# Conv half of the output projection's input normed early into its own tiles, two sums on TensorE, one more conditioning vector on GpSimd

## The chip, the cores and the metric

One NeuronCore of a Trainium2 chip runs the whole program. The metric is device time in microseconds (us) of one execution. TensorE is called PE in the profile, VectorE DVE, ScalarE ACT, GpSimd POOL and SyncE SP.

## What is computed

Two blocks of a network on x of 512 tokens and 1024 features, in float32. The change lies in the first block:

```python
cond = c_act @ ada_w[i] + ada_b[i]
shift1, scale1, gate1, shift2, scale2, gate2 = jnp.split(cond, N_MOD, axis=-1)
h = modulate(rmsnorm(x, norm1_g[i]), shift1, scale1)
u, v, val, gate = jnp.split(h @ w_in[i] + b_in[i], [D_A, 2 * D_A, 2 * D_A + D_B], axis=-1)
y_a = spatial_gating_mixer(gelu(u), gelu(v), ...)       # 512 features
y_b = conformer_conv_mixer(val, gate, ...)              # 512 features
y = jnp.concatenate([rmsnorm(y_a, out_norm_a_g[i]), rmsnorm(y_b, out_norm_b_g[i])], axis=-1)
x = x + gate1[:, None, :] * (y @ w_out[i])
h2 = modulate(rmsnorm(x, norm2_g[i]), shift2, scale2)
g_ff, up_ff = jnp.split(h2 @ w_ffn_in[i], 2, axis=-1)
x = x + gate2[:, None, :] * ((jax.nn.silu(g_ff) * up_ff) @ w_ffn_out[i])
```

At the end of the first block stands `shift_f, scale_f = split(c_act @ ada_f_w + ada_f_b)`. With the six vectors of `cond` these make eight conditioning vectors of 1024. The second block (attention, pooling, two feed-forward parts) is not touched.

## The kernel before

**Layout.** Features lie on the 128 partitions and the 512 tokens along the row, so 1024 features are 8 chunks of 128 x 512. A projection goes by blocks of 128 output features: a weight tile of 128 x 1024 is loaded (SyncE's queue, four tiles `raw` in turn), ScalarE rounds it into a high half (L293, `split_hi`), VectorE subtracts to get the low half (L297, `split_lo`), and TensorE makes three matmuls for each chunk (high x high, high x low, low x high), 24 for a block, into one of two banks in turn. The normed input has a high and a low half too. Blocks are numbered through: 0 to 15 are `w_in`, 16 to 23 `w_out`, 24 and on the first feed-forward part (`ffi0`, 44 blocks). `mm` counts blocks that TensorE has done, `wlo` splits that VectorE has done, `ev` the banks that were read out. Each engine works off its own list in the order in which the code writes it; nothing overtakes.

**Norms.** For a norm ScalarE squares each chunk, the squares are added up into one tile `ACC` (GpSimd, L575, for the norms `nb` of the conv half and `na` of the gated half; VectorE, L631, for `n2`), TensorE sums over the partitions by four matmuls with a column of ones (`pe_sum`, L476), VectorE makes the mean (L515), GpSimd the power -1/2 (L549), VectorE puts it on a diagonal (L524), and TensorE broadcasts that by a product with ones (`pe_bcast`, L493). Then, chunk by chunk, VectorE multiplies by gain and broadcast (L603), ScalarE writes the high half (L582, L584), VectorE the low half (L596, L598).

**Blocks 0 to 15** (TensorE from L1233, ScalarE from L1612, VectorE from L1976). Between the blocks stand the convolution, the group norm and the token mixing. In block 14 TensorE makes the mixing products `spatial` behind chunks 2 and 6. Ahead of block 14 stand the group-scale products (L1192), the second pair of which waits for VectorE's multiplies (L1974) of the first. In block 15 it sums `nb` behind chunk 0 and broadcasts it behind chunk 6.

**Blocks 16 and 17** (`first_two`, L1121) run staggered by three chunks, for the input is still being normed: chunks 4 to 7 (conv half, `nb`), then 0 to 3 (gated half, `na`), whose sum and broadcast stand at steps 3 and 4. Both halves are normed through the same two `TMP` tiles into `HH` and `HL`, which the blocks of `w_in` still read until block 15 is done, so the conv half is normed behind it.

**Blocks 18 to 23** (L1257, L1643, L2039). For each block VectorE splits the weight of the block after next, makes low halves for the lead blocks (`lead_low`, L2037), adds the gated result to the residual (L624), waits for its square (ScalarE, L651) and adds that to `ACC`, then does its conditioning steps.

**Lead phase** (`pe_phase_led`, L365). Blocks 24 and 25 are computed from the residual before its norm is known (`LH`, `LL`, L375 to L377); inside the first of them stand the sum for `n2` (behind chunk 2, its last part waits for the last square, L487) and its broadcast (behind chunk 6). The token factor is applied behind. Then blocks 26 and 27, staggered, read the normed chunks, and from block 28 on a loop runs.

**Conditioning vectors.** A vector is the sum of eight weight tiles (128 x 1024), each times a column of `c`: one step on VectorE for a tile (`ada_add`, L1897, L1910). `ADA_STEPS` (L39) lists how many steps VectorE does in each of its slots 0 to 15 and 16 to 23. Vectors 0 and 1 are made ahead of block 0 (L1878), 2 to 5 in these slots. Vectors 6 and 7 are made by GpSimd from the time when the lead norm is done: a load on its own queue, a product (L1019) and an addition (L1023) for each of 16 tiles, in `m_out`. For each vector TensorE sums over partitions (`ada_rows`, L1103), ScalarE copies the rows (`ada_flatten`, L1610), and TensorE turns them (`ada_turn`, L1111) into columns.

Of the kernel before, what the change touches and what calls it, by code (L numbers as in the profile page):

```python
# [14 lines left out]
F32 = mybir.dt.float32  # L15
# [23 lines left out]
ADA_STEPS = [2, 2, 1, 1, 1, 1, 1, 1, 2, 2, 2, 2, 2, 0, 0, 0] + [2, 2, 2, 2, 2, 1, 1, 0]  # L39
# [18 lines left out]
ADA_B = (ADA_N - 4) * C  # L58
ADA_C = 2 * C
PER = ADA_B // 16  # L60
# [13 lines left out]
def build_program(nc, xT, vec, ada_w, w_in, w_out, ffi, ffo, ln_rows, ws, bs, att_w, att_out, bf, pe, w1, w2,  # L74
                  pool_w, f2i, f2o, outT):
    ctx = ExitStack()
    with ctx:
# [30 lines left out]
        AE = [RAW[3][:, D:D + 2 * P], RAW[2][:, D:D + 2 * P]] + [HS[:, 0, 2 * P * i:2 * P * i + 2 * P] for i in range(2)]  # L108
# [92 lines left out]
        with ExitStack() as life:  # L201
            life.enter_context(nc.sbuf_tensor("final_lead_gap", [P, 2 * CF, S], F32))
            FLL = life.enter_context(nc.sbuf_tensor("final_lead_lo", [P, C, S], F32R))
            FSH = life.enter_context(nc.sbuf_tensor("final_shift_halves", [P, C, 2], F32R))
            FBI = life.enter_context(nc.sbuf_tensor("final_lead_bias", [P, 1], F32))
        with ExitStack() as life:
            for name, shape, dt in (("lead_gap0", [P, 14, S], F32), ("lead_hi_t", [P, C, S], F32R),
                                    ("lead_gap1", [P, 10, S], F32), ("lead_lo_t", [P, C, S], F32R),
# [68 lines left out]
        kinds = (("n1", C, 1, C - 1, C, C, C), ("nb", CA, 1, CA - 1, CA, CA, CA), ("na", CA, 1, CA - 1, CA, CA, CA),  # L277
# [87 lines left out]
        def pe_phase_led(name, hi, lo, ready, inside_lead, behind_lead, behind_first):  # L365
# [32 lines left out]
            behind_lead()  # L398
# [15 lines left out]
            behind_first()  # L414
            with nc.tensor.Fori(1, G[name]) as g:
# [531 lines left out]
        def _(pool):  # L947
# [68 lines left out]
            for i in range(ADA_C):  # L1016
                w, acc = LW[:, i % 2, :], LACC[:, i // C, :]
# [69 lines left out]
        def _(pe_):  # L1087
            def ada_sums(j, bank, sem_, count):

                pe_.wait_ge(sem_, count)  # L1090
                for k in range(C):
                    acc = (AAC[:, j % 2, :] if j < ADA_N - 2 else LACC[:, j - ADA_N + 2, :])[:, k * P:(k + 1) * P]
# [28 lines left out]
            def first_two(n, bank_count, order, ready, at=None):  # L1121

                def part(t, k, e):
                    w_h, w_l = WH[t][:, k * P:(k + 1) * P], WL[t][:, k * P:(k + 1) * P]
                    pe_.matmul(PS[t][:, :], w_h, HH[:, k, :], start=e == 0, stop=False)
                    pe_.matmul(PS[t][:, :], w_h, HL[:, k, :], start=False, stop=False)
                    return pe_.matmul(PS[t][:, :], w_l, HH[:, k, :], start=False, stop=e == C - 1)
                for step in range(C + LAG):
                    if step >= LAG:
                        if step == LAG:  # L1130
                            pe_.wait_ge(ev[1], bank_count)
                            pe_.wait_ge(wlo, n + 2)
                        m = part(1, order[step - LAG], step - LAG)
                    if at is not None:
                        at(step)
                    if step < C:
                        if step == 0:
                            pe_.wait_ge(ev[0], bank_count)
# [1346 lines left out]
```

## Time and profile before

| | us |
|---|---|
| median of three runs | 1780.65 |
| lowest, highest | 1779.13, 1781.75 |
| the profiled execution | 1781.01 |
| its span, first to last instruction | 1779.1 |
| TensorE busy | 1684.5 |
| VectorE busy | 924.3 |
| ScalarE busy | 643.8 |
| GpSimd busy | 175.4 |

The page gives shares over the whole span. For one part of the kernel the stretches, the timelines and the waits of that part are to be read: there a bracket behind an instruction says how long its engine was idle before it and which instruction ended that. The granted clock of TensorE stands in the column PEclk, 1.00 for 2.4 GHz and 0.50 for 1.2 GHz.

### The profile page before, as it was taken

To read this page: it belongs to the slowest core of one execution; us is meant where nothing else is said; L and a number is where in the kernel's file an instruction comes from. 1 tells how busy PE (TensorE), PEld (TensorE's weight loads), DVE (VectorE), ACT (ScalarE), POOL (GpSimd) and SP (SyncE) were. 2 spreads that over 40 slices of the span, in tenths; PEclk is the share of its full clock that TensorE was granted. 3 is DMA by queue.
4 is the path that set the end of the run, shared out by engine and by line. 5 is a ranking of instruction groups with operands and counts; after the bars stand their busy time and mean duration, and the time that the engine had idled before them with its cause. 6 is when DMAs were issued, how large, how long until landed. Compare 5 with 4: busy or idle time off the path is not lost.

```text
span 1779.1 us, 22325 instructions
## 1 busy us (share of the span) xinstructions
PE 1684.5 (95%) x8287; PEld 1326.9 (75%) x8287; DVE 924.3 (52%) x1390; ACT 643.8 (36%) x946; POOL 175.4 (10%) x182
## 2 busy tenths in 40 slices
PE   1999899999999999999999999999998899999996
PEld 1756678888888877666667788888887688888885
DVE  6875575453344463656667544444336644444223
ACT  1424334322333343545554444443225333333221
POOL 5001105980000020000000000002000000000000
PEclk9999899999999989999999899999999799999998
DMA  7665053542332241111102222223222122233221
GB/s 284 214 195 173 16 198 131 177 153 94 101 111 98 68 121 61 38 46 48 32 17 95 68 98 94 94 94 122 95 63 75 36 95 94 94 97 118 94 80 47
DMA packets 48587, 179.26 MB, mean 101 GB/s; under 512 B 5968, under 2 KB 6640, under 8 KB 48272
## 3 DMA queue, kind: packets, MB, share of 16 engines
q1 hardware_dynamic: 44752, 166.23, 27.7%
q0 software_dynamic: 2624, 10.59, 2.0%
q10 hardware_dynamic: 1152, 1.66, 0.4%
q8 instruction: 37, 0.61, 0.1%
q14 instruction: 22, 0.18, 0.0%
HBM read 173.04 MB, written 2.10 MB: 98 GB/s over the span
## 4 chain that ended last, share of the span: by engine, by line
PE 66%; issue 22%; DVE 8%; ACT 2%; DMA 1%; ACTq 1%; POOL 0%; DVEq 0%; POOLq 0%; SPq 0%
PE bank L358 14%; PE bank L360 14%; PE bank L359 14%; PE bank L1359 3%; PE bank L1361 2%; PE bank L1360 2%; PE bank L1467 2%; PE bank L1423 2%; PE bank L1443 2%; DVE w_lo L297 1%; DVE ada_acc L1878 1%; PE bank L1523 1%; DMA raw<-in_ada_w 1%; PE bank L1157 1%; DVE ada_acc L1910 1%
## 5 line engine op out<-in xcount | busy, mean ns | idle before, releaser
L297 DVE TENSOR_TENSOR w_lo<-raw,w_hi 128x1024 fp32r<-128x1024 f32 (+1 forms) x235 | 317.6, 1352 | 591.1 <-ACT w_hi L293 590.9
L358 PE MATMUL bank<-h_hi,w_hi 128*128 128x512 f32 x1184 | 467.5, 395 | 5.2 <-DVE k_slc L2176 1.6
L293 ACT ACTIVATE w_hi<-raw 128x1024 fp32r<-128x1024 f32 (+1 forms) x235 | 264.3, 1125 | 563.8 <-PE bank L360 472.9
L359 PE MATMUL bank<-h_lo,w_hi 128*128 128x512 f32 x1184 | 462.1, 390 | 0.0
L360 PE MATMUL bank<-h_hi,w_lo 128*128 128x512 f32 x1184 | 462.1, 390 | 0.0
L358 PEld LDWEIGHTS bank<-h_hi,w_hi 128*128 128x128 f32 x1184 | 223.0, 188 | 58.8 <-issue 7.8
L360 PEld LDWEIGHTS bank<-h_hi,w_lo 128*128 128x128 f32 x1184 | 223.0, 188 | 47.1
L359 PEld LDWEIGHTS bank<-h_lo,w_hi 128*128 128x128 f32 x1184 | 223.1, 188 | 46.1 <-issue 1.0
L358 PE MATMUL bank<-hid_hi,w_hi 128*128 128x512 f32 x528 | 205.6, 389 | 0.0
L359 PE MATMUL bank<-hid_lo,w_hi 128*128 128x512 f32 x528 | 205.4, 389 | 0.0
L360 PE MATMUL bank<-hid_hi,w_lo 128*128 128x512 f32 x528 | 205.4, 389 | 0.0
L549 POOL TENSOR_TENSOR stat<-stat,nhalf 128x4 f32<-128x4 f32 x9 | 11.9, 1320 | 1123.5 <-DVE stat L515 1123.5
L358 PEld LDWEIGHTS bank<-hid_hi,w_hi 128*128 128x128 f32 x528 | 99.1, 188 | 20.9 <-issue 0.4
L359 PEld LDWEIGHTS bank<-hid_lo,w_hi 128*128 128x128 f32 x528 | 99.1, 188 | 20.7
L360 PEld LDWEIGHTS bank<-hid_hi,w_lo 128*128 128x128 f32 x528 | 99.1, 188 | 20.5
L774 ACT ACTIVATE hid_hi<-tmp 128x512 f32 (+1 forms) x44 | 27.9, 633 | 119.7 <-DVE tmp L790 119.7
L1761 ACT ACTIVATE p_t<-bank 128x1024 f32<-128x1024 f32 (+4 forms) x52 | 37.8, 728 | 80.6 <-PE bank L1443 75.2
L1359 PE MATMUL bank<-h_hi,w_hi 128*128 128x512 f32 x128 | 58.8, 460 | 0.0
L1778 ACT ACTIVATE scores<-scores,att_stat 128x512 f32<-128x512 f32 (+3 forms) x96 | 52.7, 552 | 11.1 <-DVE att_stat L2270 11.1
L771 ACT ACTIVATE tmp<-tmp 128x512 f32<-128x512 f32 x44 | 27.8, 632 | 71.1 <-DVE tmp L783 71.1
L792 DVE TENSOR_TENSOR hid_lo<-tmp,hid_hi 128x512 f32 (+1 forms) x44 | 30.5, 693 | 39.4 <-ACT hid_hi L774 39.4
L1361 PE MATMUL bank<-h_hi,w_lo 128*128 128x512 f32 x128 | 50.4, 394 | 0.0
(381 smaller groups left out, 2022.6 us busy)
## 6 DMA issues: line engine op xcount, KB each, us to landing
raw<-in_f2i SPq DMA_DIRECT2D x88, 512.0 KB, 3.2
raw<-in_ffi SPq DMA_DIRECT2D x44, 512.0 KB, 3.3
raw<-in_f2o SPq DMA_DIRECT2D x32, 704.0 KB, 4.0
ada_w<-in_ada_w SPq DMA_DIRECT2D x32, 512.0 KB, 4.2
raw<-in_att_w SPq DMA_DIRECT2D x23, 512.0 KB, 3.3
raw<-in_ffo SPq DMA_DIRECT2D x16, 704.0 KB, 4.1
raw<-in_ada_w SPq DMA_DIRECT2D x16, 512.0 KB, 5.0
raw<-in_w_in SPq DMA_DIRECT2D x16, 512.0 KB, 5.3
```

The source lines that it names most:

```text
L293: nc.scalar.activation(WH[par][:, 0:kc * P], RAW[s][:, 0:kc * P], ACT.Copy).then_inc(whi, count)
L297: nc.vector.tensor_tensor(WL[par][:, 0:kc * P], RAW[s][:, 0:kc * P], WH[par][:, 0:kc * P].bitcast(F32), ALU.subtract).then_inc(wlo, count)
L358: pe_.matmul(bank[:, :], w_h, hi[:, k0 + k, :], start=start and k == 0, stop=False)
L359: pe_.matmul(bank[:, :], w_h, lo[:, k0 + k, :], start=False, stop=False)
L360: last = pe_.matmul(bank[:, :], w_l, hi[:, k0 + k, :], start=False, stop=stop and k == kc - 1)
L1359: pe_.matmul(PS[t][:, :], w_h, hi[:, k, :], start=first, stop=False)
L1360: pe_.matmul(PS[t][:, :], w_h, lo[:, k, :], start=False, stop=False)
L1361: m = pe_.matmul(PS[t][:, :], w_l, hi[:, k, :], start=False, stop=last)
L1423: m = pe_.matmul(QB[:, half, 0:L], lhs, rhs, start=kind != "fox", stop=True)
L1443: m = pe_.transpose(TB[:, half, j * P:(j + 1) * P], sc[:, j * P:(j + 1) * P], IDN[:, :])
L1761: act.activation(dst[:, :, 0:L], TB[0:rows, :, 0:L], ACT.Copy).then_inc(a6["pt"], 1)
L1778: act.activation(sc, sc, ACT.Exp, scale=-1.0, bias=AST[:, 0, col:col + 1], accum_out=AST[:, 1, col:col + 1]).then_inc(a6["ex"], 1)
```

## The change

- **Conditioning.** VectorE makes 24 steps instead of 32: none in slot 12, and 1, 2, 2, 1 in slots 16 to 19. Vector 5 (second gate) joins 6 and 7 on GpSimd, with tiles of its own (`LATE`), so GpSimd makes 24 steps, after a clearing of one more tile. Its row sum stands in the middle of `ffi0`, and its flattening and turn with those of 6 and 7 at the end. The flattened rows of vectors 5 to 7 go to parts of `h_scratch`, the space of the low halves.
- **Conv half.** It gets tiles of its own, `NBH` and `NBL`, so that its norming starts in block 14. GpSimd adds only the first two of its squares, and TensorE sums three tiles (`pe_sum_parts`) behind chunk 5 of block 14, and broadcasts behind chunk 0 of block 15. For the gated half GpSimd adds three squares and TensorE sums two tiles.
- **Blocks 16 and 17.** TensorE goes: block 16 chunks 4, 5, 6; sum `na`; block 17 chunks 4, 5, 6; chunk 7; broadcast `na`; chunk 7 of 17; turn 3; then chunks 0 to 3, staggered by two.
- **Blocks 18 to 23.** VectorE adds the residual first, then makes the lead low halves (two in each of slots 4, 5 and 6, two behind), then the steps, then the addition to `ACC`.
- **Lead phase.** The split of block 26 moves behind the first normed chunk on ScalarE and behind the third on VectorE; block 26's SiLU moves ahead of the lead hidden chunk's high half.
- ScalarE loads the GELU table by a GELU of one column ahead of the gated squares.

```diff
-ADA_STEPS = [2, 2, 1, 1, 1, 1, 1, 1, 2, 2, 2, 2, 2, 0, 0, 0] + [2, 2, 2, 2, 2, 1, 1, 0]
+ADA_STEPS = [2, 2, 1, 1, 1, 1, 1, 1, 2, 2, 2, 2, 0, 0, 0, 0] + [1, 2, 2, 1, 0, 0, 0, 0]
...
-        kinds = (("n1", C, 1, C - 1, C, C, C), ("nb", CA, 1, CA - 1, CA, CA, CA), ("na", CA, 1, CA - 1, CA, CA, CA),
+        kinds = (("n1", C, 1, C - 1, C, C, C), ("nb", CA, 1, 1, CA, CA, CA), ("na", CA, 1, 2, CA, CA, CA),
...
+        def pe_sum_parts(nj_, squares, count):
+            nc.tensor.wait_ge(n_acc, nj_.acc_end)
+            nc.tensor.wait_ge(n_sq, nj_.sq + count)
+            parts = [ACC] + squares
+            for e, part in enumerate(parts):
+                for i in range(TC):
+                    m = nc.tensor.matmul(NS[:, i:i + 1], part[:, i * P:(i + 1) * P], ONE[:, 0:1],
+                                         start=e == 0 and i == 0, stop=e == len(parts) - 1 and i == TC - 1,
+                                         skip_group_check=True)
+            m.then_inc(n_used, 1)
...
-            for q, sq in (("nb", lambda k: Y[:, k, 0:S]), ("na", sq_p1)):
-                pool_sum(nj[q], CA, sq)
-                pool_rsqrt(nj[q])
+            pool_sum(nj["nb"], 2, lambda k: Y[:, k, 0:S])
+            pool_rsqrt(nj["nb"])
+            pool_sum(nj["na"], 3, sq_p1)
+            pool_rsqrt(nj["na"])
             pool_rsqrt(nj["n2"])
-            pool.wait_ge(ada_row, 4)
+            pool.wait_ge(ada_row, 3)
+            pool.wait_ge(mm, N0["ffi0"] + 2)
             pool.wait_ge(n_lo, nj["n2"].lo + C)
+            chain(pool.memset(LATE[0], 0.0))
             chain(pool.memset(LACC, 0.0))
...
+                if n == 14 and k == 5:
+                    pe_sum_parts(nj["nb"], [Y[:, 2, 0:S], Y[:, 3, 0:S]], CA)
                 if n == 15 and k == 0:
-                    pe_sum(nj["nb"])
-                if n == 15 and k == 6:
                     pe_.wait_ge(j1["gx"], CA)
                     pe_bcast(nj["nb"], PS[4])
...
+            for k in range(CA, C - 1):
+                pe_.wait_ge(n_lo, nj["nb"].lo + k - CA + 1)
+                out_part(0, k)
+            pe_sum_parts(nj["na"], [sq_p1(3)], CA)
+            pe_.wait_ge(ev[1], O0["w_out"] // 2)
+            pe_.wait_ge(wlo, n_out + 2)
+            for k in range(CA, C - 1):
+                out_part(1, k)
+            pe_.wait_ge(n_lo, nj["nb"].lo + CA)
+            out_part(0, C - 1)
+            pe_bcast(nj["na"])
+            out_part(1, C - 1)
+            ada_turn(3)
+            for step in range(CA + 2):
+                if step < CA:
+                    pe_.wait_ge(n_lo, nj["na"].lo + step + 1)
+                    m = out_part(0, step)
+                    if step == CA - 1:
+                        m.then_inc(mm, 1)
+                if step >= 2:
+                    m = out_part(1, step - 2)
...
+                    act.activation(R32[:, 0, 0:1], ONE[:, 0:1], ACT.Gelu)
+                    gated_square(0)
+                    gated_square(1)
                 if n == 15:
-                    act_squares(nj["na"], 3, lambda k: YA[:, k, :], lambda k: act.wait_ge(j1["ya"], k + 1), sq_p1)
+                    conv_hi(0)
+                    conv_hi(1)
+                    gated_square(2)
+                    conv_hi(2)
...
-            act_parts(nj["nb"], CA, k0=CA, behind=last_square)
+            split_hi(17, 1, 1, C, ROUND["w_out"])
+            gated_square(3)
+            conv_hi(3)
             act_parts(nj["na"], CA)
...
                     gated(0)
                     gated(1)
+                    dve_diag(nj["nb"], DA)
                     mixed(2)
                     mixed(3)
+                    dve.wait_ge(n_rb, nj["nb"].turn)
+                    conv_normed(0)
+                    conv_normed(1)
                 if n == 15:
-                    dve_diag(nj["nb"], DA)
+                    conv_low(0)
+                    conv_normed(2)
                     gated(2)
+                    conv_low(1)
...
-            dve_parts(nj["nb"], CA, lambda k: CV[:, k, :], lambda k: vcol("on_b", k), k0=CA, bank=PS[4], between=beside,
-                      before_low=lambda: gated(3))
-            dve_diag(nj["na"], DA)
+            gated(3)
+            conv_normed(3)
+            conv_low(2)
+            dve_mean(nj["na"], DA)
+            split_lo(17, 1, 1, C)
+            conv_low(3)
+            dve_diag(nj["na"], DA, mean=False)
...
-                for k in {C - 3: (0,), C - 2: (1, 2), C - 1: (3, 4, 5, 6)}.get(n, ()):
+                dve_gated(nj["n2"], "w_out", (n, N0["w_out"] + n + 1), n % 2, 16, last=True)
+                for k in {4: (0, 1), 5: (2, 3), 6: (4, 5)}.get(n, ()):
                     if k == 0:
                         dve.wait_ge(mod_ready, 6)
                     lead_low(k)
-                dve_gated(nj["n2"], "w_out", (n, N0["w_out"] + n + 1), n % 2, 16, last=n == C - 1)
                 if n < C - 1:
                     ada_step(16 + n)
+                    dve.wait_ge(n_sq, nj["n2"].sq + n + 1)
+                    dve.wait_ge(n_acc, nj["n2"].acc + n + 1)
+                    dve.tensor_tensor(ACC, ACC, TMP[:, n % 2, :], ALU.add).then_inc(n_acc, 1)
+            lead_low(C - 2)
             lead_low(C - 1)
```

## Rows read from the trace of the kernel before

**Rows 1.** The page, busy time of each engine, its share and instructions

```profile
PE 1684.5 (95%) x8287; PEld 1326.9 (75%) x8287; DVE 924.3 (52%) x1390; ACT 643.8 (36%) x946; POOL 175.4 (10%) x182
```

**Rows 2.** Stretches: length, busy us (instructions) of PE, PEld, DVE, ACT, POOL; PEclk; DMA

```profile
171.90:175.30 3.40, 3.40 (x9) 2.72 (x9) 0.69 (x1) 3.40 (x7) 0.60 (x1) 0.51 0.48 155
190.60:195.80 5.20, 2.22 (x11) 1.34 (x9) 5.09 (x7) 3.71 (x6) 1.61 (x2) 0.99 0.01 2
195.80:206.00 10.20, 8.82 (x23) 6.17 (x22) 3.05 (x6) 0.63 (x1) 1.02 (x1) 0.50 0.00 0
209.40:212.80 3.40, 3.40 (x9) 2.64 (x8) 3.13 (x8) 1.03 (x2) 0.00 (x0) 0.50 0.00 0
256.60:260.60 4.00, 1.07 (x9) 1.07 (x10) 2.69 (x5) 1.75 (x3) 0.00 (x0) 1.00 0.00 0
260.60:264.00 3.40, 3.40 (x9) 2.62 (x10) 2.42 (x6) 0.60 (x2) 2.06 (x1) 0.50 0.16 41
```

**Rows 3.** Timeline of TensorE: start, us, what; idle before it and who ended it

```profile
169.99 1.95 PE L1192 MATMUL bank<-sig,selg 8*128 8x512 f32 x4 [1.96 <-DVE conv L1974]
...
200.09 1.70 PE L476 MATMUL bank<-ones,tmp 128*128 128x1 f32 x8
...
204.36 1.83 PE L493 MATMUL bank<-tmp,ones 128*128 128x512 f32 x2
...
218.23 0.50 PE L358 MATMUL bank<-h_hi,w_hi 128*128 128x512 f32 x1 [1.09 <-DVE x_res L624]
...
252.97 0.50 PE L375 MATMUL bank<-lead_hi_t,w_hi 128*128 128x512 f32 x1
...
259.53 1.05 PE L487 MATMUL bank<-ones,tmp 128*128 128x1 f32 x8 [2.95 <-ACT tmp L651]
...
288.94 0.49 PE L358 MATMUL bank<-h_hi,w_hi 128*128 128x512 f32 x1 [1.29 <-ACT tmp L761]
```

**Rows 4.** Waits from 160 to 292 us: total us, times, longest

```profile
PE bank L1125 <- DVE h_lo L596: 6.6, 4, 2.2
```

**Rows 5.** A stretch of the first feed-forward phase, columns as in rows 2

```profile
294.00:390.00 96.00, 96.00 (x426) 79.47 (x425) 47.13 (x34) 28.53 (x35) 89.97 (x45) 1.00 0.50 170
```

**Rows 6.** Timeline of VectorE

```profile
222.07 1.22 DVE L297 TENSOR_TENSOR w_lo<-raw,w_hi 128x1024 fp32r<-128x1024 f32 x1
...
224.65 0.69 DVE L631 TENSOR_TENSOR tmp<-tmp 128x512 f32<-128x512 f32 x1 [0.70 <-ACT tmp L651]
...
225.26 2.66 DVE L1910 SCALAR_TENSOR_TENSOR ada_acc<-ada_w,c_act,ada_acc 128x1024 f32<-128x1024 f32 x2
...
227.84 1.22 DVE L297 TENSOR_TENSOR w_lo<-raw,w_hi 128x1024 fp32r<-128x1024 f32 x1
...
255.42 2.73 DVE L2037 SCALAR_TENSOR_TENSOR lead_lo_t<-x_res,gs,lead_hi_t 128x512 fp32r<-128x512 f32 x4
...
258.07 0.75 DVE L624 SCALAR_TENSOR_TENSOR x_res<-bank,mod,x_res 128x512 f32<-128x512 f32 x1
```

**Rows 7.** Timeline of ScalarE

```profile
173.42 2.18 ACT L566 ACTIVATE y_pad<-conv 128x512 f32<-128x512 f32 x4
...
190.75 0.69 ACT L1632 ACTIVATE u_act<-bank,vec_sb 128x512 f32<-128x512 f32 x1 [1.74 <-PE bank L360]
```

**Rows 8.** Timeline of GpSimd

```profile
261.10 2.06 POOL L549 TENSOR_TENSOR stat<-stat,nhalf 128x4 f32<-128x4 f32 x1 [58.01 <-DVE stat L515]
...
283.16 1.81 POOL L1010 MEMSET m_out<- 128x2048 f32 x1 [20.00 <-DVE h_lo L598]
```

**Rows 9.** By line: 294 to 390 us, then VectorE's split from 400 to 496

```profile
L1019 POOL TENSOR_SCALAR m_out<-m_out,c_act 128x1024 f32<-128x1024 f32 x16 | 48.0, 3002 | 3.9 <-DMA m_out<-in_ada_w 3.2
...
L1023 POOL TENSOR_TENSOR m_out<-m_out 128x1024 f32<-128x1024 f32 x15 | 38.3, 2556 | 1.3
...
L297 DVE TENSOR_TENSOR w_lo<-raw,w_hi 128x1024 fp32r<-128x1024 f32 x18 | 32.7, 1818 | 41.9 <-ACT w_hi L293 41.9
...
L297 DVE TENSOR_TENSOR w_lo<-raw,w_hi 128x1024 fp32r<-128x1024 f32 x18 | 22.1, 1226 | 55.9 <-ACT w_hi L293 55.9
```

More of the change, by code:

```diff
@@ L57 @@
 ADA_A = 2 * C
-ADA_B = (ADA_N - 4) * C
-ADA_C = 2 * C
-PER = ADA_B // 16
+ADA_L = 3
+ADA_B = (ADA_N - 2 - ADA_L) * C
+ADA_C = ADA_L * C
 R_P1 = ADA_A // 4
@@ L107, in build_program @@
         SEL4 = sb("row_group", [P, 4])
[L108 removed]
+        AE = [RAW[3][:, D:D + 2 * P]] + [HS[:, i // 2, 2 * P * (i % 2):2 * P * (i % 2) + 2 * P] for i in range(ADA_L)]
         ACC = TMP2[:, 0, :]
@@ L201, in build_program @@
         with ExitStack() as life:
+            life.enter_context(nc.sbuf_tensor("late_gap", [P, 20, S], F32))
+            LATE = [life.enter_context(nc.sbuf_tensor("late_acc", [P, D], F32))[:, :], LACC[:, 0, :], LACC[:, 1, :]]
+        with ExitStack() as life:
             life.enter_context(nc.sbuf_tensor("final_lead_gap", [P, 2 * CF, S], F32))
@@ L213, in build_program @@
                     LH = t_
+                elif name == "conv_hi":
+                    NBH = t_
+                elif name == "conv_lo":
+                    NBL = t_
                 elif name == "lead_lo_t":
@@ L363, in block, with pe_phase_led @@
             last.then_inc(mm, 1)
-        def pe_phase_led(name, hi, lo, ready, inside_lead, behind_lead, behind_first):
+        def pe_phase_led(name, hi, lo, ready, inside_lead, midway):
             pe_, n, cnt = nc.tensor, N0[name], O0[name] // 2
@@ L413, in pe_phase_led @@
             m.then_inc(mm, 1)
-            behind_first()
-            with nc.tensor.Fori(1, G[name]) as g:
+            with nc.tensor.Fori(1, G[name] // 2 + 1) as g:
+                for t in range(4):
+                    up(g, t)
+            midway()
+            with nc.tensor.Fori(G[name] // 2 + 1, G[name]) as g:
                 for t in range(4):
@@ L1119, in _, with part, first_two @@
             ada_sums(1, PS[5], raw_used, 2 * C)
[L1121 to L1127, printed above, removed]
+            def part(t, k, hi, lo, first, last):
+                w_h, w_l = WH[t][:, k * P:(k + 1) * P], WL[t][:, k * P:(k + 1) * P]
+                pe_.matmul(PS[t][:, :], w_h, hi, start=first, stop=False)
+                pe_.matmul(PS[t][:, :], w_h, lo, start=False, stop=False)
+                return pe_.matmul(PS[t][:, :], w_l, hi, start=False, stop=last)
+            def first_two():
                 for step in range(C + LAG):
@@ L1130, in first_two, with out_chunk, out_part, out_block @@
                         if step == LAG:
[L1131 to L1135, printed above, removed]
+                            pe_.wait_ge(ev[1], 1)
+                            pe_.wait_ge(wlo, 2)
+                        k = step - LAG
+                        m = part(1, k, HH[:, k, :], HL[:, k, :], k == 0, k == C - 1)
                     if step < C:
                         if step == 0:
-                            pe_.wait_ge(ev[0], bank_count)
-                            pe_.wait_ge(wlo, n + 1)
-                        pe_.wait_ge(n_lo, ready + step + 1)
-                        m0 = part(0, order[step], step)
+                            pe_.wait_ge(ev[0], 1)
+                            pe_.wait_ge(wlo, 1)
+                        pe_.wait_ge(n_lo, nj["n1"].lo + step + 1)
+                        m0 = part(0, step, HH[:, step, :], HL[:, step, :], step == 0, step == C - 1)
                         if step == C - 1:
                             m0.then_inc(mm, 1)
+                m.then_inc(mm, 1)
+            def out_chunk(k):
+                return (HH[:, k, :], HL[:, k, :]) if k < CA else (NBH[:, k - CA, :], NBL[:, k - CA, :])
+            def out_part(t, k):
+                hi, lo = out_chunk(k)
+                return part(t, k, hi, lo, k == CA, k == CA - 1)
+            def out_block(n):
+                pe_.wait_ge(ev[n % 2], O0["w_out"] // 2 + n // 2)
+                pe_.wait_ge(wlo, N0["w_out"] + n + 1)
+                for k in (4, 5, 6, 7, 0, 1, 2, 3):
+                    m = out_part(n % 2, k)
                 m.then_inc(mm, 1)
@@ L1677, in _ @@
             phase_splits("ffi0", act, act_step, lambda g, t: act_ffi("ffi0", ff[0], g, t), first=1)
-            ada_flatten(6)
-            ada_flatten(7)
+            act.wait_ge(ada_row, ADA_N - 2)
+            for j in range(ADA_N - ADA_L, ADA_N):
+                ada_flatten(j)
             act.wait_ge(coef, 1)
```

73 lines of the change are left out of this document (37 added, 36 removed).

## Prediction

> **What bounds the kernel now.** I read the page's shares first: TensorE is busy for 95% of the span [rows 1], so only its idle time and its time at half clock can be won. The changed lines run between about 163 and 290 us, so the second view is the table by stretches over that part [rows 2]. Its PEclk column shows three stretches of 3.4 us and one of 10.2 at 0.50 to 0.51, the 1.2 GHz level (2.4 GHz is the other), and two stretches in which TensorE is mostly idle: 2.98 us of 190.6 to 195.8 and 2.93 of 256.6 to 260.6. The third view is TensorE's order of time, where a bracket names who ended a gap [rows 3], with its waits by releaser [rows 4]. The gaps form four knots:
> - 1.96 us before the second pair of group-scale products, for a convolution multiply on VectorE;
> - four inside the first two output blocks, 6.6 us together, for normed low halves;
> - 1.09 us before the third output block, for a residual update;
> - 2.95 us inside the first lead block, for the last square, and 1.29 us behind the lead phase, for a SiLU.
> In three places the clock is at half right behind such gaps.
>
> **Unit prices.** In 96 us of a quiet stretch TensorE starts 426 matmuls of 512 columns [rows 5]: 0.225 us each, 0.68 a chunk of three, 5.44 a block of 24 with its start. At half clock all take twice that. At half clock four one-column sums took 1.70 us and a broadcast 1.83 [rows 3]; at full clock I count 0.8 and 0.9.
>
> **1. Group scales and block 14 (-2.0).** Two conditioning steps, 2.66 us [rows 6], leave VectorE's slot 12, ahead of the multiply that TensorE waits for; the gap of 1.96 goes. The half clock behind it, 3.4 us [rows 2], costs 1.7; without a gap before it I take it as gone (bounds 0 and -1.7). Against this, the conv half's sum takes three passes in block 14 instead of one in block 15: 2 x 0.8 = +1.6 (at half clock +3.4). Nobody waits for it: ScalarE's four squares are done by 175.6 [rows 7] and TensorE gets there at about 176. So block 15 ends at 188.6 instead of 190.6.
>
> **2. First two output blocks (-2.3).** They last from 190.6 to 217.1 (218.23 less its gap of 1.09 [rows 3]), 26.5 us. I rebuilt the new order from the same durations. Work: 16 chunks 10.9, two passes of the sum 1.6, broadcast 0.9, the third vector's turn 0.4 = 13.8. Waits:
> - Chunks 4 and 5 are ready. Chunk 6 stands on VectorE behind the last gating, and that behind ScalarE's last GELU, 0.69 us [rows 7], which starts when block 15 ends and two of ScalarE's own pieces are done, at about 189.5. Then gating, norming and low half, 0.7 each: 192.2. TensorE is ready at 190.0: 2.3 idle.
> - VectorE then waits for the gated half's mean ahead of the split of block 17. Queued behind that mean are the split (1.22 [rows 6]) and chunk 7; so TensorE, done with the sum at 194.7, waits for the split to 196.2: 1.5.
> - After the broadcast, gated chunk 0 needs norming, high and low half, 2.2 us as now [rows 4], of which one chunk and the turn hide 1.0: 1.2 idle. Chunks 1 and 2 come 1.4 us apart (two VectorE pieces each) and take 0.68: 0.7 + 0.7.
> Work and idle 20.2, with semaphores 20.5. These gaps are as dense as the present ones, which were followed by 10.2 and 3.4 us at half clock [rows 2]. I take 7.4 us in place of those 13.6, for there is less idle time in a row; that costs 3.7 (bounds 0 and 6.8). 24.2 against 26.5: -2.3.
>
> **3. Output blocks 18 to 23 (-1.4).** From 218.23 to 252.97 [rows 3] they take 34.7 us; six blocks and the row sums (0.5) need 33.1. VectorE's cycle from split to split is 5.77, with 2.6 for two conditioning steps and 0.70 of waiting for the square [rows 6]. The addition moves behind the conditioning, which hides that wait, and the steps fall from 2,2,2,2,2,1,1 to 1,2,2,1,0,0,0: at most 5.1 us, below TensorE's 5.44. Two lead low halves in each of slots 4 to 6 cost 1.4, and there no step is left: also below. The 1.09 before block 18 stays, since its split, low half and residual must still follow block 16 beside three chunks. -1.4 (bounds -1.6 and 0).
>
> **4. Lead phase (-5.1).** The last residual stands behind four lead low halves of 0.7 us and starts 5.1 us behind block 23 (252.97 to 258.07 [rows 3, 6]). Put first, its square is ready 1.6 us behind the block, before TensorE has done its three chunks and the first pass: -2.95. The half clock behind the gap (3.4 us [rows 2]) goes too: -1.7. But the broadcast now becomes due sooner: mean, power on GpSimd at 2.06 [rows 8] and diagonal end 0.45 after TensorE wants it. That is -4.2. The splits of the first full blocks move behind their first chunks and keep pace within 0.4. Behind the phase ScalarE does the SiLU of block 2 without waiting for the lead hidden chunk: -1.29. Row sum 5 and turn 5 (0.6 and 0.4) move to the middle of the phase and behind it at the same price. -4.2 + 0.4 - 1.3 = -5.1.
>
> **5. GpSimd (0).** It takes 24 late steps instead of 16. A step is a product of 3.00, an addition of 2.56 and a DMA issue, with gaps 6.5 [rows 9]; 24 take 156. It now starts clearing at 283.16 [rows 8]; some 10 us earlier, behind one more clearing of 0.9, the first step starts at about 281 and the last ends at 437. TensorE asks for the last at about 495, for the first eight (333) at about 386. What grows is the time beside VectorE, whose weight split takes 1.82 us instead of 1.23 while GpSimd works [rows 9]; TensorE still works 96 of 96 us there, VectorE being busy for only 47 [rows 5]. Eight steps more prolong the same state. The eight 512 KB loads move with them from SyncE's queue, where they stand among the output weights, to GpSimd's; SyncE still waits for slot 16's first step before the load of block 21, four blocks ahead of its use.
>
> **Sum.** -2.0 - 2.3 - 1.4 - 5.1 = -10.8. The profiled execution took 1781.01 us, 1.9 around its span of 1779.1: 1770.2. The median of the three runs is 0.4 lower, so 1769.8, rounded to **1770.0**. About 0.2%, 3.6 us, can be told from no change here.
>
> **Rivals.**
> - A, the clock holds through the gaps of part 2. For it, it was still at 0.99 over 190.6 to 195.8 with 2.98 us idle; against it, the 10.2 us at half right behind [rows 2]. Another -3.7: **1766.3**. Chance 0.14.
> - B, the wait only moves: chunk 6 waits longer behind ScalarE's queue, which now holds squares, high halves, GELU and a split in series, and block 17's split with it, at half clock nearly throughout. Part 2 gives nothing, and block 14 keeps half of its slow stretch: -10.8 + 2.3 + 0.9: **1773.0**. For it, that chain of four engines has no slack in my order; against it, low half 7 is the only one added to it. 0.18.
> - C, the edit does not bring the lead phase forward: its first block waits for low halves 6 and 7 or for the diagonal instead of the square. Of 4.2 us some 1 remains: **1773.0**. Against it, VectorE is idle there. 0.07.
> - D, slower: GpSimd becomes the bound. If a late step takes over (495 - 281) / 24 = 8.9 us, TensorE waits at the last row sum, and each us more per step costs 24. At 10 us per step it is 521, +26 - 10.8: **1795**. Against it, 6.5 us per step [rows 9]. 0.04.
> The forecast has 0.53; 0.04 is left for none of these.
>
> The Trainium skill's SBUF — State Buffer, section "Who interferes with whom", has the rule that speaks for D: a VectorE instruction with two SBUF inputs and a GpSimd one that reads SBUF exclude each other, and the loser "fully blocks" for the whole instruction. The trace agrees in direction, the 1.82 against 1.23. With GpSimd always the loser, two splits of 1.23 would stretch a step from 6.5 to 9.0 and by that rule alone the sum would be about -9 (end at 497 against 495) instead of -10.8.
>
> **Range.** 1764.5 to 1776.0: A with the lower bounds, B or C together with part 3 at nothing. Faster 0.88 (forecast, A, B and C, less for several misses at once), within 0.2% 0.07, slower 0.05.
>
> **What would show it.** Right: the wait for the conv multiply and the half clock at 172 gone; a gap of about 2.3 us for a low half behind 188 and one of 1.5 for the weight split behind the sum; blocks 18 to 23 at 5.44 to 5.5; no gap for the square in the lead block; GpSimd's last late step before 450. Wrong: any TensorE wait for a late vector, block 17 ending after 214.5, or part 4 under 3 us.

## The result, and the profile after

The changed kernel takes **1771.66 us** (median of 5 runs, 1769.51 to 1773.27), the kernel before 1780.65 in the runs beside them (1779.13 to 1781.75): a ratio of 0.9945 [0.9933, 0.9957], 9.0 us less. The profiled execution took 1770.52 us with a span of 1768.7, against 1781.01 and 1779.1 before: 10.5 less. Its own run is 1.1 below its median and the profiled one of before 0.4 above, hence the 1.5 between the two differences.

The page of the kernel after, busy time by engine; it answers to [rows 1]:

```profile
PE 1681.7 (95%) x8311; PEld 1326.2 (75%) x8311; DVE 922.4 (52%) x1382; ACT 644.5 (36%) x947; POOL 221.7 (13%) x204
```

TensorE has 24 one-column products more and is still busy 2.8 us less, since it does less of its work at half clock (the tables below). GpSimd has 46 us more, nearly all of it the eight late steps. Next the table by stretches of the kernel after, columns as in [rows 2]:

```profile
178.20:181.60 3.40, 3.40 (x22) 2.65 (x23) 1.82 (x2) 0.00 (x0) 2.26 (x2) 0.51 0.00 0
189.85:195.20 5.35, 3.17 (x19) 2.46 (x17) 2.38 (x4) 3.67 (x6) 1.28 (x1) 1.00 0.13 51
195.20:202.00 6.80, 5.32 (x18) 4.49 (x19) 2.59 (x4) 0.00 (x0) 1.93 (x1) 0.51 0.01 2
166.95:214.44 47.49, 40.73 (x222) 30.89 (x221) 26.88 (x40) 21.07 (x32) 6.57 (x5) 0.89 0.07 23
214.44:248.00 33.56, 33.56 (x152) 27.21 (x153) 26.71 (x31) 15.23 (x21) 0.00 (x0) 1.00 0.45 157
248.01:277.70 29.69, 29.34 (x152) 23.80 (x150) 20.55 (x31) 14.46 (x20) 5.47 (x4) 1.00 0.17 54
294.00:390.00 96.00, 96.00 (x429) 78.91 (x429) 46.73 (x36) 28.71 (x36) 89.63 (x46) 1.00 0.52 175
```

And the same three stages, from row sum 3 to block 18, to the lead phase and to block 28, in the kernel before:

```profile
167.39:218.23 50.84, 41.21 (x197) 29.92 (x196) 28.33 (x43) 20.92 (x31) 9.52 (x8) 0.83 0.13 43
218.23:252.97 34.74, 34.66 (x152) 26.80 (x153) 30.03 (x32) 13.44 (x20) 0.00 (x0) 1.00 0.68 234
252.97:288.94 35.97, 31.73 (x162) 26.07 (x163) 24.86 (x36) 16.82 (x25) 5.21 (x4) 0.95 0.21 69
```

The stages fall by 3.35, 1.17 and 6.28 us. With 0.44 already there at row sum 3 (166.95 against 167.39) block 28 starts 11.24 us earlier; 0.8 is given back later, where row sum 5 and its turn now stand. The 0.44 can't be put down to the change: in a second profiled execution of it (below) row sum 3 starts at 167.57, and TensorE has 3.4 us at half clock at 138.2, where this one has none. In the first stage the clock was at 1.2 GHz (0.51) for 3.4 and 6.8 us, 10.2 in all, where it was for 17.0 before [rows 2]. From block 18 to block 28 it is at 2.4 GHz throughout.

TensorE's order of time in the kernel after: start, length, what, and in brackets the idle time before it and who ended it, as in [rows 3]:

```profile
166.95 0.64 PE L1128 MATMUL bank<-ada_acc,ones 128*32 128x256 f32 x8
167.52 1.98 PE L1231 MATMUL bank<-sig,selg 8*128 8x512 f32 x4
...
175.76 0.95 PE L496 MATMUL bank<-ones,tmp 128*128 128x1 f32 x8
176.57 2.04 PE L496 MATMUL bank<-ones,y_pad 128*128 128x1 f32 x16
...
193.55 0.50 PE L1148 MATMUL bank<-conv_hi,w_hi 128*128 128x512 f32 x1 [2.17 <-DVE conv_lo L2039]
...
198.37 0.76 PE L1148 MATMUL bank<-conv_hi,w_hi 128*128 128x512 f32 x1 [1.48 <-DVE w_lo L305]
...
206.20 0.50 PE L1148 MATMUL bank<-h_hi,w_hi 128*128 128x512 f32 x1 [1.20 <-DVE h_lo L618]
...
254.82 0.39 PE L385 MATMUL bank<-lead_hi_t,w_lo 128*128 128x512 f32 x1
255.36 1.12 PE L515 MATMUL bank<-tmp,ones 128*128 128x512 f32 x2
...
277.70 0.41 PE L366 MATMUL bank<-h_hi,w_hi 128*128 128x512 f32 x1
```

The scale products follow the row sum with no bracket, where 1.96 stood. The three passes of the conv half's sum run from 175.76. The knot of the first two output blocks has other names: a conv low half, the weight split, a gated low half. The lead phase shows no wait for a square, and block 28 (277.70) has no bracket.

### The profile page after: what moved, and what is told of

Same layout as the page of the kernel before. It is cut to its first block, busy times and chain, and to the rows that moved or that the text cites. A ratio compares the mean times of both kernels' runs of the same rounds, so it can differ in the third digit from the quotient of the medians.

```text
span 1768.7 us, 22382 instructions
## 1 busy us (share of the span) xinstructions
PE 1681.7 (95%) x8311; PEld 1326.2 (75%) x8311; DVE 922.4 (52%) x1382; ACT 644.5 (36%) x947; POOL 221.7 (13%) x204
## 4 chain that ended last, share of the span: by engine, by line
PE 68%; issue 22%; DVE 6%; ACT 1%; DMA 1%; ACTq 1%; POOL 0%; POOLq 0%; DVEq 0%; SPq 0%
PE bank L366 14%; PE bank L368 14%; PE bank L367 14%; PE bank L1417 3%; PE bank L1419 2%; PE bank L1418 2%; PE bank L1525 2%; PE bank L1481 2%; PE bank L1501 2%; DVE ada_acc L1946 1%; PE bank L1148 1%; PE bank L1149 1%; PE bank L1581 1%; PE bank L1150 1%; DVE w_lo L305 1%
## 5 line engine op out<-in xcount | busy, mean ns | idle before, releaser
L366 PE MATMUL bank<-h_hi,w_hi 128*128 128x512 f32 x1136 | 447.2, 394 | 2.7 <-DVE k_slc L2263 1.6
L368 PE MATMUL bank<-h_hi,w_lo 128*128 128x512 f32 x1136 | 442.4, 389 | 0.0
L367 PE MATMUL bank<-h_lo,w_hi 128*128 128x512 f32 x1136 | 442.4, 389 | 0.0
L366 PEld LDWEIGHTS bank<-h_hi,w_hi 128*128 128x128 f32 x1136 | 213.3, 188 | 53.1 <-issue 6.4
L368 PEld LDWEIGHTS bank<-h_hi,w_lo 128*128 128x128 f32 x1136 | 213.4, 188 | 44.7
L367 PEld LDWEIGHTS bank<-h_lo,w_hi 128*128 128x128 f32 x1136 | 213.4, 188 | 43.8 <-issue 1.0
L1044 POOL TENSOR_SCALAR m_out<-m_out,c_act 128x1024 f32<-128x1024 f32 x24 | 70.8, 2950 | 3.8 <-DMA m_out<-in_ada_w 2.8
L1417 PE MATMUL bank<-h_hi,w_hi 128*128 128x512 f32 x128 | 58.8, 460 | 0.0
```

Of the source, the lines that this page charges most:

```text
L366: pe_.matmul(bank[:, :], w_h, hi[:, k0 + k, :], start=start and k == 0, stop=False)
L367: pe_.matmul(bank[:, :], w_h, lo[:, k0 + k, :], start=False, stop=False)
L368: last = pe_.matmul(bank[:, :], w_l, hi[:, k0 + k, :], start=False, stop=stop and k == kc - 1)
L1044: pool.tensor_scalar(w, w, CACT[:, i % C:i % C + 1], None, ALU.mult).then_inc(late_mul, 1)
L1417: pe_.matmul(PS[t][:, :], w_h, hi[:, k, :], start=first, stop=False)
```

## The experiments

They ran in three groups of four, each group on one chip with runs of the kernel before beside it; a ratio is against those. A gap is a bracket of TensorE's order of time, a stage is one of the three above.

### What the knot of the first two blocks hangs on, and what the three passes cost

**Order of the queue alone: the split of block 17 ahead of the gated half's mean.**

```diff
-            dve_mean(nj["na"], DA)
             split_lo(17, 1, 1, C)
             conv_low(3)
-            dve_diag(nj["na"], DA, mean=False)
+            dve_diag(nj["na"], DA)
```

> Against the changed kernel only VectorE's order behind block 15 differs: split of block 17 and conv low half 7 come before the mean of the gated half. Theory (the 1.48 us wait of TensorE stands in VectorE's queue behind the mean): that wait goes, block 18 starts 1.5 us earlier, up to 2.5 if less of the stretch falls to half clock; about 1769. Rival (the wait only moves to the broadcast, whose diagonal now comes later): block 18 starts within 0.5 us of where it does.

1771.34 us (4 runs, 1770.21 to 1773.95), 0.9948 [0.9931, 0.9965]: the time of the change. The gap of 1.48 is gone from TensorE's timeline, but the profiled execution was its slowest run and has more half clock than the change's. Its table by stretches:

```profile
178.40:185.20 6.80, 6.80 (x42) 5.54 (x42) 3.30 (x4) 0.00 (x0) 2.25 (x2) 0.50 0.00 0
195.50:205.70 10.20, 10.16 (x32) 8.72 (x33) 2.58 (x4) 0.04 (x1) 1.02 (x1) 0.50 0.01 2
```

17.0 us at 1.2 GHz where the change has 10.2, and the first stage takes 49.80 instead of 47.49. A wait was taken away and no time with it. Inconclusive for the gap's own worth: in this execution the clock took more than the gap gave.

**The same, and low half 6 ahead of the last gating.**

```diff
+            conv_low(2)
             gated(3)
             conv_normed(3)
-            conv_low(2)
-            dve_mean(nj["na"], DA)
             split_lo(17, 1, 1, C)
             conv_low(3)
-            dve_diag(nj["na"], DA, mean=False)
+            dve_diag(nj["na"], DA)
```

> As split_first, and conv low half 6 is also taken ahead of the last gating. Theory (the 2.17 us wait of TensorE is also only the place in the queue; the high half it needs is there 2.2 us earlier): chunk 6 starts at about 191.7 instead of 193.55, the sum then waits for the last square, about 0.5; together with the split -2.9 us for the start of block 18, and up to -5 if TensorE stays at 2.4 GHz. Rival (the chain over GELU, gating and square sets the time): no more than split_first.

1767.77 us (4 runs, 1767.54 to 1770.35), 0.9935 [0.9918, 0.9951]. Repeated on another chip:

> The changed kernel with conv low half 6 ahead of the last gating and the split of block 17 and low half 7 ahead of the mean, once more with more rounds. Theory: 2.5 to 4 us below the change (1768 to 1769.5), with gaps of 0.9 and 0.4 in place of 2.2 and 1.5, row sum 3 to block 18 at 44.4 where 6.8 us of it are at half clock. Rival (the first time was a lucky position of the stretches at half clock): 1771 or more.

1767.94 us (5 runs, 1765.77 to 1768.25), 0.9925 [0.9911, 0.9938]. TensorE's gaps in the repetition, up to block 18:

```profile
192.93 0.50 PE L1148 MATMUL bank<-conv_hi,w_hi 128*128 128x512 f32 x1 [0.91 <-DVE conv_lo L2039]
...
194.28 1.02 PE L496 MATMUL bank<-ones,tmp 128*128 128x1 f32 x8 [0.39 <-ACT u_act L1644]
...
203.74 0.51 PE L1148 MATMUL bank<-h_hi,w_hi 128*128 128x512 f32 x1 [1.19 <-DVE h_lo L618]
```

0.91 and 0.39 in place of 2.17 and 1.48: 2.35 us less idle. The stretch from the scale products to block 18 takes 43.84 us instead of 46.92, 3.1 less: besides the idle time TensorE is busy 0.73 less (39.43 against 40.16), for the half clock behind the gaps is 3.4 instead of 6.8. So 2.17 was an order of the queue for more than half: the low half was ready to be made, and stood behind a gating that waits for the GELU. This is the version that beats both kernels. Against the kernel before it gains 12.2 and 13.8 us on the two chips (1779.96, 1781.73). The change itself was not run beside it; the nearest kernels that were, the one with only the split moved (1771.34) and the one with refilled slots at the end of this section (1771.08), are 3.6 and 3.1 slower.

**GpSimd sums all four squares, TensorE makes one pass.**

```diff
-("nb", CA, 1, 1, CA, CA, CA)
+("nb", CA, 1, CA - 1, CA, CA, CA)
...
-            pool_sum(nj["nb"], 2, lambda k: Y[:, k, 0:S])
+            pool_sum(nj["nb"], CA, lambda k: Y[:, k, 0:S])
...
-                if n == 14 and k == 5:
-                    pe_sum_parts(nj["nb"], [Y[:, 2, 0:S], Y[:, 3, 0:S]], CA)
+                if n == 14 and k == 6:
+                    pe_sum(nj["nb"])
```

> Against the changed kernel GpSimd adds all four conv squares again and TensorE sums one tile, behind the second pair of mixing products in block 14. Theory (the three passes cost TensorE about 1.9 us and, being nearly idle time for its array, bring the 3.4 us at half clock in block 14): block 15 ends 1.9 us earlier, and 3.3 if the half clock goes too; norming still starts in time. Rival (GpSimd's additions are late, which is why the passes were put in): TensorE waits for the sum or the diagonal, no gain or a loss of up to 1 us.

1771.32 us (4 runs, 1769.63 to 1772.82), 0.9947 [0.993, 0.9963]: no difference. What the two passes gave, a new wait takes. The timelines of this kernel, TensorE's, then VectorE's and GpSimd's around 180 us:

```profile
185.97 1.10 PE L515 MATMUL bank<-tmp,ones 128*128 128x512 f32 x2 [1.74 <-DVE tmp L546]
```

```profile
177.49 3.00 DVE L2031 TENSOR_TENSOR v_act<-v_act,u_act 128x512 f32<-128x512 f32 x2
...
184.07 1.76 DVE L546 TENSOR_TENSOR tmp<-ident,stat 128x512 f32<-128x512 f32 x1 [1.13 <-POOL stat L571]
```

```profile
177.35 1.09 POOL L597 TENSOR_TENSOR tmp<-y_pad 128x512 f32<-128x512 f32 x1 [15.08 <-ACT y_pad L588]
178.58 3.04 POOL L597 TENSOR_TENSOR tmp<-y_pad,tmp 128x512 f32<-128x512 f32 x2
...
184.00 1.27 POOL L597 TENSOR_TENSOR tmp<-u_act 128x512 f32<-128x512 f32 x1
```

The additions end at 181.6, later than the squares that TensorE can sum itself, so mean, power and diagonal come late and TensorE waits 1.74 for the broadcast. Beside them two gatings take 3.00 us on VectorE, where they take 1.28 in the kernel before. The three passes of the change are paid for by an earlier sum: a draw.

**Both together.**

> low_and_split and one_pass together. If both theories hold, block 18 starts 5 to 8 us earlier than in the changed kernel and the kernel takes 1764 to 1767 us; if only the queue order counts, about 1769; if neither, 1771.7.

1769.0 us (4 runs, 1766.37 to 1769.34), 0.9933 [0.9916, 0.9949]: the queue's order without the passes taken away has the same (0.9935). The passes are worth nothing here either.

### Where the gain sits

**The change again,** unaltered, on the chip of the next three:

> The changed kernel once more, unaltered, as the level for the other three on this chip. Both theories: about 0.9945 of the kernel before. Its profile says how far the position of the stretches at half clock differs between two executions of one program; by the theory that they follow low activity but begin at times of their own, block 18 starts within 2 to 3 us of 214.44, with the same gaps in front of it.

1772.12 us (5 runs, 1771.39 to 1773.55), 0.9955 [0.9942, 0.9969]. Its stages are 47.49, 33.58 and 29.70, within 0.02 those of the first profile.

**The kernel before with one edit of the change:** VectorE's order in blocks 18 to 23 (residual, lead low halves, steps, addition).

```diff
-                for k in {C - 3: (0,), C - 2: (1, 2), C - 1: (3, 4, 5, 6)}.get(n, ()):
+                dve_gated(nj["n2"], "w_out", (n, N0["w_out"] + n + 1), n % 2, 16, last=True)
+                for k in {4: (0, 1), 5: (2, 3), 6: (4, 5)}.get(n, ()):
...
-                dve_gated(nj["n2"], "w_out", (n, N0["w_out"] + n + 1), n % 2, 16, last=n == C - 1)
                 if n < C - 1:
                     ada_step(16 + n)
+                    dve.wait_ge(n_sq, nj["n2"].sq + n + 1)
+                    dve.wait_ge(n_acc, nj["n2"].acc + n + 1)
+                    dve.tensor_tensor(ACC, ACC, TMP[:, n % 2, :], ALU.add).then_inc(n_acc, 1)
+            lead_low(C - 2)
             lead_low(C - 1)
```

> The kernel before with one edit of the change: in blocks 16 to 23 VectorE does the residual first, then the lead low halves (slots 4 to 6 and behind), the steps, and last the addition to the sum of squares. 32 steps stay on VectorE. Theory (the last residual's place in the queue made the lead gap): the wait of 2.95 for the square and the 3.4 us at half clock behind it go, the lead phase is 4 us shorter, blocks 18 to 23 about 1 us; in all -5, about 1775. Rival (without moving the steps, slots 4 to 6 overfill VectorE and it falls behind): -2 or less, with TensorE waiting for a split or a residual in those blocks.

1774.31 us (5 runs, 1772.24 to 1774.53), 0.9962 [0.9948, 0.9975]. These few lines give 6.2 of the 8.4 us that the change gives on this chip (1780.55 less 1774.31 and 1772.12). The stages say which: 50.81, 33.58 and 31.48, the first as before, the second as after, the third without the gap for the square but with 1.3 left before block 28.

**The change with that edit undone.**

> The changed kernel with VectorE's old order in blocks 16 to 23 (low halves ahead of the residual, the addition right behind it). Theory: the lead gap of about 3 us and the half clock come back, +4 to +5 us against the change, although VectorE has 8 steps less. Rival (the steps taken off VectorE were what freed it): +1 or less.

1778.25 us (10 runs, 1775.57 to 1781.68), 0.9988 [0.9978, 0.9997]: 6.1 more than the change, the counterpart of the 6.2. From its timeline of TensorE and its table by stretches:

```profile
234.16 0.64 PE L1128 MATMUL bank<-ada_acc,ones 128*32 128x256 f32 x8 [1.90 <-DVE ada_acc L1978]
...
257.31 1.05 PE L509 MATMUL bank<-ones,tmp 128*128 128x1 f32 x8 [1.07 <-ACT tmp L673]
```

```profile
234.90:238.30 3.40, 3.40 (x9) 2.69 (x10) 1.69 (x3) 1.24 (x2) 0.00 (x0) 0.52 0.43 154
258.80:262.20 3.40, 3.40 (x10) 2.66 (x9) 2.00 (x3) 0.17 (x2) 2.06 (x1) 0.52 0.30 83
```

Two waits, and behind each 3.4 us at 1.2 GHz. Here all the rest of the change (early norm, moved steps, lead splits) is worth only 2.3 us.

**The change with the lead phase's splits and SiLU in the old place** (on VectorE `split_lo` of block 26 at chunk 0 again; ScalarE's part:)

```diff
+            split_hi(N0["ffi0"] + 2, 0, 2, C, ROUND["ffi0"])
...
-                    split_hi(N0["ffi0"] + 2, 0, 2, C, ROUND["ffi0"])
...
-            act_ffi("ffi0", ff[0], 0, 2)
             act.wait_ge(lead_hid, 1)
             act.activation(FH[:, 0, :], TMP2[:, 0, :], ACT.Copy).then_inc(ff[0]["hid_hi"], 1)
+            act_ffi("ffi0", ff[0], 0, 2)
```

> The changed kernel with the old lead order: split of block 26 ahead of the first normed chunk on ScalarE and behind it on VectorE, and the lead hidden chunk's high half ahead of block 26's SiLU. Theory: the gap of 1.29 before block 28 comes back, and because the broadcast is now early, the split blocks both queues until the first lead block is done, so TensorE also waits 1 to 2 us for low halves: +2.3 to +3.3. Rival (the broadcast is early enough for either order): +1.3 only.

1774.78 us (7 runs, 1774.0 to 1777.5), 0.9969 [0.9957, 0.9981]: 2.7 more than the change. The one new gap on TensorE, in its timeline:

```profile
280.07 0.49 PE L366 MATMUL bank<-h_hi,w_hi 128*128 128x512 f32 x1 [1.64 <-ACT tmp L783]
```

The third stage is longer by 1.80, nearly all of it this wait for the SiLU. The wait for a low half inside the phase stayed at 0.20: in the profile moving the splits has no share that can be seen, the SiLU's place has it all. The runs' 2.7 are 0.9 more than the stage shows; where these are, no trace says.

**The kernel before with both edits,** order and lead phase:

> The kernel before with the new VectorE order of blocks 16 to 23 and the new order of splits and SiLU in the lead phase; the conv half, the sums and the conditioning vectors stay as before. Theory (these reorderings are worth 1.2 + 4.5 + 1.3 or a little more, the rest of the change 2 to 3): 1772.5 to 1774, lead phase about 30 us, the part ahead of block 18 unchanged at 50.8. Rival (the lead order needs the row sum and turn moved away): no better than the reordering of the blocks alone.

1771.07 us (5 runs, 1770.39 to 1774.4), 0.995 [0.9936, 0.9963]. **By the medians two reorderings of queues give the time of the whole change,** with all 32 conditioning steps on VectorE and the conv half normed where it was. Its profiled execution was the slowest of the five, 3.3 above the median, with stages of 50.87, 33.57 and 30.08: the last two are nearly the change's, the first is the old one. Its knot is the old one too, gaps of 1.93, 1.04, 1.43 and 2.23 for low halves, and its table still has the old half clock:

```profile
195.90:206.10 10.20, 8.77 (x23) 6.18 (x22) 3.12 (x6) 0.63 (x1) 1.02 (x1) 0.50 0.00 0
209.60:213.00 3.40, 3.40 (x9) 2.65 (x9) 3.15 (x8) 1.05 (x2) 0.00 (x0) 0.51 0.00 0
```

### What the conditioning steps that left VectorE were worth

Two kernels give VectorE the weight of such steps back as extra pieces that add zero times an input; nothing that is computed changes. The piece is

```diff
+            def extra_step(acc, w):
+                dve.scalar_tensor_tensor(acc, w, 0.0, acc, ALU.mult, ALU.add).then_inc(more, 1)
```

**Two in slot 12** (on `X[:, 0:2, :]`):

> The changed kernel with two more VectorE pieces of a conditioning step's size (128 x 1024, two inputs in SBUF, adding zero times the input) in slot 12, where the change took two away. Theory (those steps stand ahead of the multiply that the second pair of group scales waits for, but the stretch at half clock near there comes in any case, as it did in every run so far): the gap of about 2 us returns, row sum 3 to block 18 takes 49.4 us instead of 47.5, and no more stretches at half clock. Rival (the prediction's: the gap also makes the stretch at half clock): +3.6.

1776.36 us (6 runs, 1773.62 to 1777.96), 0.9972 [0.996, 0.9984]: 4 to 5 us slower than the change. TensorE's timeline and the table by stretches:

```profile
169.97 1.95 PE L1232 MATMUL bank<-sig,selg 8*128 8x512 f32 x4 [1.88 <-DVE conv L2062]
```

```profile
171.80:175.20 3.40, 3.40 (x9) 2.68 (x9) 0.69 (x1) 3.40 (x7) 0.52 (x1) 0.51 0.46 154
182.10:188.90 6.80, 6.80 (x42) 5.53 (x42) 3.30 (x4) 0.00 (x0) 2.26 (x2) 0.50 0.00 0
199.20:209.40 10.20, 8.72 (x28) 7.58 (x29) 2.59 (x4) 0.00 (x0) 1.93 (x1) 0.50 0.01 2
```

The old gap returns, 1.88 against 1.96, so the steps in slot 12 were its cause. But the stage from row sum 3 to block 18 takes 54.20 us, 6.7 longer than the change's: 1.9 is the gap, and 4.8 come behind it, where 20.4 us are at half clock against 10.2. Both theories (+1.9, +3.6) were too low for this profile, which is of the slowest of the six runs; the median's 4 to 5 are nearer to the second.

**Slots 16 to 22 refilled to the old 2,2,2,2,2,1,1** (a second piece in slots 16 and 19, two, one and one in 20 to 22):

> The changed kernel with VectorE's slots 16 to 22 filled up to the number of pieces of before (2,2,2,2,2,1,1), the new order kept. Theory (the new order alone brought VectorE's cycle below TensorE's 5.44, and the residual comes first in each slot): block 18 to the lead phase stays at 33.6 us within 0.2 and the lead phase at 29.7; the steps moved to GpSimd buy nothing here. Rival (VectorE's load counts): +1 to +2 in these two stretches.

1771.08 us (4 runs, 1769.2 to 1772.42), 0.9946 [0.993, 0.9961], the change's ratio. Blocks 18 to 23 take 34.28 us, 0.7 more, of which 0.64 is one wait for row sum 4 (`231.81`, released by `ada_acc`); the lead phase is unchanged. That wait belongs to the change's own list, in which the last step of vector 4 stands in slot 19 and in the kernel before in slot 17. The kernel before with the new order does all 32 steps on VectorE and takes 33.58 us for these blocks, without a wait.

## Why the prediction was right, and where a term was off

The time, its sign and the forecast case held: 1771.66 against 1770.0, by the medians a gain of 9.0 us where 10.7 was forecast. Part by part, in the profiled executions:

| part | predicted | measured |
|---|---|---|
| 1. scales, block 14 | -2.0 | -0.3, and -0.4 from before row sum 3, no part of the change |
| 2. first two blocks | -2.3 | -3.1 |
| 3. blocks 18 to 23 | -1.4 | -1.2 |
| 4. lead phase | -5.1 | -5.3 |
| 5. GpSimd | 0 | 0 |
| sum | -10.8 | -10.5 (0.2 of it elsewhere) |

That the sum is only 0.3 off is luck in part: what part 1 lacks (1.7) is made up by the 0.8 more of part 2 and by the 0.4 and 0.2 that no part had foreseen.

**1 was the term that failed.** The gap of 1.96 went and the two passes came: from 175.76 to 178.5 they and the first took 2.7 instead of 0.8, +1.9 against the +1.6 predicted. "Without a gap before it I take it as gone" was wrong: the 3.4 us at half clock did not go, they stood at 178.2 instead of 171.9, right behind the one-column sums. That no gap is needed shows the table by stretches of the kernel with one pass, ahead of its scale products:

```profile
142.00:163.30 21.30, 21.30 (x98) 15.94 (x98) 13.42 (x23) 10.33 (x14) 1.45 (x1) 0.97 0.44 148
163.40:166.80 3.40, 3.40 (x10) 2.63 (x9) 3.40 (x5) 0.69 (x1) 0.00 (x0) 0.52 0.36 116
```

TensorE is busy for 21.30 of 21.30 us, and then the 3.4 us at half clock come at 163.4, behind the first pair of scale products (8 rows); none comes at 178 there, nor in the change with the old block order, which has its own at 163.2 and all three passes. So -1.7 was booked for a slow stretch that did not go with the gap. That it only changes its place is the likely reading, not a shown one: with the gap put back (slot 12 loaded) there is a stretch behind the gap, at 171.8, and another at 182.1.

**2** was right in what waits and in the size: gaps of 2.17, 1.48, 1.20, 0.41 and 0.41 against 2.3, 1.5, 1.2, 0.7 and 0.7, half clock 6.8 against 7.4. The 0.8 more came from the two last gaps and the clock. Rival B (part 2 gives nothing) and A (the clock holds) are both out. What I did not see is that 2.17 and 1.48 are mostly a matter of the queue: low half 6 and the split of block 17 depend on nothing that they stood behind.

**3 and 4** held: 5.5 us a block and 0.6 for the row sum (33.56 in all), with no gap left; the wait for the square gone with its half clock, the broadcast 0.3 late (255.36, where 0.23 behind the matmul of 254.82 would be 255.05) where I had 0.45, no wait before block 28, and 1.0 for row sum and turn 5 moved behind the stage (that is the -5.3 of the 6.28). The steps that left slots 16 to 22 have no part in it that the time shows (refilled, 0.9946), nor one that the profiles show: with all 32 steps and the new order the blocks take 33.58. The prediction gave the falling number of steps a share in part 3; the order has it all. Rival C (the lead phase waits for something else) is out.

**5** held: the last late step ends at 436.3 against 437, row sum 5 starts at 386.63 and the last one at 496.24 without waiting, and TensorE is busy for 96.00 of 96 us beside it. D, the slower case, is out: fifteen products in 96 us are 6.4 us a step, where 8.9 would have made TensorE wait. In the kernel after, grouped by line from 294 to 390 us, these answer to [rows 9]:

```profile
L305 DVE TENSOR_TENSOR w_lo<-raw,w_hi 128x1024 fp32r<-128x1024 f32 x18 | 32.1, 1786 | 41.5 <-ACT w_hi L301 41.5
...
L1044 POOL TENSOR_SCALAR m_out<-m_out,c_act 128x1024 f32<-128x1024 f32 x15 | 44.0, 2934 | 0.7
```

The split stays at 1.79 us, against 1.82 in [rows 9]: eight steps more prolong the state and do not deepen it.

**The sum held, but the medians do not divide it as the profiles do.** The lines of the profiles add up (-3.35, -1.17, -6.28). By the medians, reordering two queues gives the ratio of the whole change, 0.995 [0.9936, 0.9963] against 0.9945 and 0.9955, so that the early norm and the moved steps show no share beside these two edits; the intervals leave room for 2 or 3 us. Profile against profile they do show one: with the two reorderings the profiled execution took 1774.40 us, 3.0 and 3.9 more than the two of the change, and its first stage is 3.4 longer. Its five runs were 1774.40, 1774.32, 1771.07 twice and 1770.39, at a mean granted clock of 0.972 and 0.973 in the first two and 0.975 to 0.976 in the others. So the clock differs between executions of one program by as much as this share, as it does in the two profiles of the change at 138.2; in which stage the three shorter runs had less of the half clock, no trace shows.

Slot 12 does not settle it. Two pieces put back there cost 4 to 5 us, but the kernel with the two reorderings also has two steps in that slot and the gap of 1.96, and takes 1771.07 on the same chip. What the early norm is worth alone was not tried, and stays open.

## What to carry to other kernels

Where the bound engine waits for a short piece on an in-order queue, look first at what stands ahead of that piece and is needed by nobody soon: here moving such pieces gave 6.2 us with a few lines, 2.7 with the place of one SiLU, and 3 to 4 more in the improved version, while handing steps of blocks 16 to 22 to another engine gave nothing that the runs can tell. Price a gap with the half clock that is seen behind it, but book no gain for a slow stretch that stands among products of few rows or columns, since it may come back at another place; and take more than one execution before a difference of 3 us is read from profiles.

## What the runs showed of the hardware

- **A slow stretch without a gap.** In the change TensorE is busy without idle time from 167.5 to 189 (21.50 of 21.50 us, clock 0.92), and still has 3.4 us at 1.2 GHz at 178.2. In every one of the fourteen traces at least one such stretch stood among the products of 8 rows, the mixing products and the one-column sums: at 163, at 171 to 172 (there always behind a gap of 1.9), at 178 to 179 or at 182. At 178 with the split moved, and at 182 with slot 12 loaded, it was 6.8 long.
- **Extra clock loss.** One gap of 1.88 put back into the change went with 4.8 us in the stage behind it: the clock was then at half for 20.4 us instead of 10.2, also at 182 and 199, far behind the gap. One execution can't say how much of it the gap brings each time. The median of six runs is 4 to 5 us above the change, more than the gap, so part of it is no accident of the profiled one; but the kernel with the two reorderings has such a gap and 17.0 us at half clock, and is no slower than the change.
- **VectorE beside GpSimd.** Two gatings of 128x512 take 1.28 us alone (the kernel before), 2.10 where one GpSimd addition of 1.09 starts just ahead (the change) and 3.00 beside three (GpSimd sums all four squares); the diagonal 0.69 alone and 1.76 beside an addition of 1.27. The diagonal starts 0.07 behind the addition, and 1.07 more is about the rest of it. By the Trainium skill's SBUF — State Buffer, section "Who interferes with whom", such a pair exclude each other for a whole instruction. The diagonal's 1.07 more agrees with it. The weight split has 0.56 more (1.79 against 1.23), beside a GpSimd busy for 89.63 of 96 us; waiting out half of a GpSimd instruction of 2.5 to 2.9 us each time would be 1.3 more, an estimate, so it has less than that rule would give. GpSimd is hardly held up at all: its product takes 2.93 on average and 2.85 at the shortest.
